# Late modulation in a transformer layer: the selecting matmul of each of 16 units is taken out, and the partial sums are added once by VectorE

## The reference

```
mod = silu(c) @ w_ada + b_ada                  # c: 1 prompt row and 8 sample rows, w_ada [1024, 6*1024]
sh1, sc1, gt1, sh2, sc2, gt2 = split(mod, 6)
h = rms_norm(x, norm1_g) * (1 + sc1) + sh1
proj = h @ w_in                                # retention q,k,v,g; attention q,k,v; gates
... retention (4 heads), differential attention (8 heads)
merged = gate_ret * (ret_o @ w_br_ret) + gate_diff * (diff_o @ w_br_diff)
x = x + gt1 * (merged @ w_out)
h2 = rms_norm(x, norm2_g) * (1 + sc2) + sh2
x = x + gt2 * hierarchical_moe(h2)
```

## Time and profile before

| what | value |
|---|---|
| three runs | 1525.07, 1530.54, 1531.76 us |
| median | 1530.54 us |
| profiled execution, first to last instruction | 1524.3 us |
| PE busy | 1495.9 us (98%), 7974 matmuls |
| DVE, ACT, POOL busy | 818.2, 652.8, 297.2 us |
| granted TensorE clock, mean | 0.998 |
| DMA | 301.88 MB, mean 198 GB/s |

### The profile page before, as it was taken

How to read it: one execution, slowest core, us unless ns; L and a number is a source line. 1 busy time by engine, 2 the same in 40 slices (tenths; PEclk the granted TensorE clock), 3 DMA queues, 4 the chain that set the end, 5 groups by cost and what they waited for, 6 DMA issues and landing times.

```text
span 1524.3 us, 21822 instructions
## 1 busy us (share of the span) xinstructions
PE 1495.9 (98%) x7974; PEld 1136.4 (75%) x7974; DVE 818.2 (54%) x1440; ACT 652.8 (43%) x1073; POOL 297.2 (19%) x177
## 2 busy tenths in 40 slices
PE   8999999999999999999999999999999999999998
PEld 6775777577757775778787667777788988887885
DVE  4332341234123412321585867755465799998998
ACT  5323211321232123312345454555333388888883
POOL 2342134213421342133100000000231100001004
PEclk9999999999999999999999999999999999999999
DMA  9545454645464546432432245134861699999996
GB/s 349 185 141 172 162 172 148 180 161 171 146 184 156 174 145 187 141 99 80 171 100 95 70 140 194 42 129 150 278 186 42 203 360 400 393 392 391 406 398 234
DMA packets 150221, 301.88 MB, mean 198 GB/s; under 512 B 16555, under 2 KB 44379, under 8 KB 149989
## 3 DMA queue, kind: packets, MB, share of 16 engines
q1 hardware_dynamic: 146310, 290.01, 55.4%
q0 software_dynamic: 3808, 10.49, 2.0%
HBM read 257.84 MB, written 45.77 MB: 199 GB/s over the span
## 4 chain that ended last, share of the span: by engine, by line
PE 44%; DMA 3%; DVE 2%; issue 1%; ACT 1%; POOL 0%; DVEq 0%; ACTq 0%; SPq 0%; POOLq 0%
PE pj L93 11%; PE pj L95 11%; PE pj L94 11%; PE d_B L2685 1%; DMA d_kc<-cache_diff_k 1%; PE d_B L2712 1%; PE d_B L2704 1%; DMA m_raw<-w 1%; PE d_B L2746 1%; PE d_B L2694 1%; PE d_B L2852 1%; PE d_B L2673 1%; PE d_B L1717 1%; PE pj L1709 0%; PE d_B L2723 0%
## 5 line engine op out<-in xcount | busy, mean ns | idle before, releaser
L93 PE MATMUL pj<-ring_hi,hT_hi 128*128 128x512 f32 x880 | 368.2, 418 | 3.0 <-ACT d_q_rows L2147 2.1
L95 PE MATMUL pj<-ring_hi,hT_lo 128*128 128x512 f32 x880 | 345.1, 392 | 0.0
L94 PE MATMUL pj<-ring_lo,hT_hi 128*128 128x512 f32 x880 | 344.4, 391 | 0.0
L511 POOL TENSOR_TENSOR ring_lo<-ring_raw,ring_hi 128x1024 fp32r<-128x1024 f32 x79 | 191.1, 2423 | 495.2 <-ACT ring_hi L585 495.2
L585 ACT ACTIVATE ring_hi<-ring_raw 128x1024 fp32r<-128x1024 f32 x79 | 83.3, 1057 | 362.3 <-DMA ring_raw<-w_in 349.5
L1577 DVE TENSOR_TENSOR m_lo<-m_raw,m_hi 128x1024 fp32r<-128x1024 f32 x188 | 221.9, 1220 | 17.2 <-ACT m_hi L1483 16.1
L93 PEld LDWEIGHTS pj<-ring_hi,hT_hi 128*128 128x128 f32 x880 | 166.1, 189 | 45.8 <-issue 12.4
L1483 ACT ACTIVATE m_hi<-m_raw 128x1024 fp32r<-128x1024 f32 x188 | 191.5, 1057 | 18.0 <-DMA m_raw<-w 14.9
L95 PEld LDWEIGHTS pj<-ring_hi,hT_lo 128*128 128x128 f32 x880 | 165.5, 188 | 36.7
L94 PEld LDWEIGHTS pj<-ring_lo,hT_hi 128*128 128x128 f32 x880 | 166.5, 189 | 28.4 <-issue 1.0
L782 DVE SCALAR_TENSOR_TENSOR r_S<-r_S,g,r_sm 128x512 f32<-128x512 f32 x64 | 45.0, 744 | 135.4 <-PE r_sm L1031 135.4
(11 more groups left out here) (386 smaller groups left out, 2410.9 us busy)
## 6 DMA issues: line engine op xcount, KB each, us to landing
m_raw<-w SPq DMA_DIRECT2D x188, 512.0 KB, 9.9
ring_raw<-w_in SPq DMA_DIRECT2D x72, 512.0 KB, 3.5
r_S<-state_ret SPq DMA_DIRECT2D x64, 256.0 KB, 4.5
r_ada_raw<-w_ada SPq DMA_DIRECT2D x16, 1024.0 KB, 6.6
o_state_s<-r_S SPq DMA_DIRECT2D x64, 256.0 KB, 4.3
a_raw<-w_ada SPq DMA_DIRECT2D x8, 1024.0 KB, 12.3
ring_raw<-w_in SPq DMA_DIRECT2D x32, 256.0 KB, 3.4
ring_raw<-w_br_ret SPq DMA_DIRECT2D x16, 512.0 KB, 4.2
```

The costliest lines, as they stand in the source:

```text
L93: pe.matmul(out, s_hi, m_hi, start=start, stop=False)
L94: pe.matmul(out, s_hi, m_lo, start=False, stop=False)
L95: return pe.matmul(out, s_lo, m_hi, start=False, stop=stop)
L511: pool.tensor_tensor(lo[:, p], raw[:, p], hi[:, p].bitcast(F32), ALU.subtract).then_inc(lo_done, 1)
```

## The change

- The job SP and all its parts go: the matmul `spread`, VectorE's `take_spread`, the 9 KB stores, and the two small loads of each unit (bias row, norm2_g).
- ACT copies all 128 rows of the unit's bank. SP stores these 128 x 256 partial sums to a scratch tensor (128 KB for each unit). ACT's copy of unit u waits for the store of unit u-2, which used the same buffer.
- SP sends the last unit behind the load of DQ0's piece 0. Behind the load of piece 1 it reads the partial sums back as 72 rows x 4 x 512 and loads b_ada and norm2_g nine times each, in 18 small DMAs (`load_parts`). GpSimd has filled the tile of factors with ones.
- VectorE adds the four strips and the bias in 5 operations of 72x512 (`sum_parts`), ahead of its five products for GR1. SP stores the result once, behind the load of DQ0's piece 3 (`store_mods`).
- The later phases read the same values from another layout. The tiles spr and g2 go, and some tiles lie elsewhere.

```diff
     def unit():
         u = next(ada)
-        return [("AD", u)], [("SP", u)]
+        return [("AD", u)]
...
-            ad, sp = unit()
-            jobs += ad + [("U", h - 1, u) for u in range(8, 16)] + sp
+            jobs += unit() + [("U", h - 1, u) for u in range(8, 16)]
             jobs += [("O", h - 1, t) for t in range(NT)]
             pieces.append(f"BR{h - 1}")
             banks += [(f"BR{h - 1}a", five), (f"BR{h - 1}b", five)]
-            for _ in range(2):
-                ad, sp = unit()
-                jobs += ad + sp
+            jobs += unit() + unit()
         if h == RH:
             break
-        ad, sp = unit()
-        jobs += ad + sp + [("T", h, t) for t in ROPE_ORDER]
+        jobs += unit() + [("T", h, t) for t in ROPE_ORDER]
...
-        spr = sb("r_spread", [P, 2, UW], F32)
-        g2 = sb("r_g2", [P, 2, UW], F32)
         uraw = sb("r_ada_raw", [P, KT, UW], F32)
+        sb.at = K.phase_base + 106496
...
+        MR = 9 * 4 * D_MODEL // W
+        parts = nc.alloc_sbuf_tensor_at("r_mod_parts", [P, NH, W], F32, offset=at_oT)
+        mod_add = nc.alloc_sbuf_tensor_at("r_mod_add", [P, W], F32, offset=at_oT + 8192)
+        mod_by = nc.alloc_sbuf_tensor_at("r_mod_by", [P, W], F32, offset=at_oT + 10240)
...
-                if u >= 2:
-                    job_taken(sp, "SP", u - 2)
-                sp.dma_start(mod[P - 1:P, u % 2], io["b_ada"][:, unit_cols(u)]).then_inc(ub_in[u % 2], 16)
-                c = unit_cols(u).start % D_MODEL
-                sp.dma_start(g2[0:9, u % 2], io["norm2_g"][:, c:c + UW].broadcast_to([9, UW])).then_inc(ub_in[u % 2], 16)
+
+            parts_home = io["mods"][1].rearrange("s p d -> (s p d)")
 
             def send_unit(u):
-                job_taken(sp, "SP", u)
-                seg, c = unit_cols(u).start // D_MODEL, unit_cols(u).start % D_MODEL
-                sp.dma_start(io["mods"][0, seg - 2, 0:9, c:c + UW], spr[0:9, u % 2]).then_inc(m_out[u % 2], 16)
+                job_taken(sp, "AD", u)
+                home = parts_home.rearrange("(p c) -> p c", p=P)
+                sp.dma_start(home[:, u * UW:(u + 1) * UW], mod[:, u % 2]).then_inc(m_out[u % 2], 16)
+
+            def load_parts():
+                for i in range(2):
+                    sp.wait_ge(m_out[i], 16 * NU // 2)
+                bank_done(sp, f"BR{RH - 1}b", NT - 1)
+                sp.wait_ge(by_set, 1)
+                home = parts_home.rearrange("(j p c) -> p j c", j=NH, c=W)
+                sp.dma_start(parts[0:MR], home[0:MR]).then_inc(parts_in, 16)
+                add = io["b_ada"][:, 4 * W:].rearrange("o (q c) -> (o q) c", c=W)
+                by = io["norm2_g"].rearrange("o (q c) -> (o q) c", c=W)
+                for r in range(9):
+                    sp.dma_start(mod_add[8 * r:8 * r + 8], add).then_inc(parts_in, 16)
+                    sp.dma_start(mod_by[8 * r + 4:8 * r + 6], by).then_inc(parts_in, 16)
+
+            def store_mods():
+                sp.wait_ge(mod_sum, 5)
+                sp.dma_start(io["mods"][0].rearrange("s p d -> (s p d)").rearrange("(p c) -> p c", c=W)[0:MR], mod_add[0:MR]).then_inc(mods_out, 16)
...
+                    elif was == "GR1":
+                        if p == 0:
+                            send_unit(NU - 1)
+                        elif p == 1:
+                            load_parts()
+                        elif p == 3:
+                            store_mods()
...
-            send_unit(NU - 1)
             sp.wait_ge(Sp_out, RH * 32)
             for i in range(2):
                 sp.wait_ge(S_out[i], 64 * 2 * RH)
-                sp.wait_ge(m_out[i], 16 * NU // 2)
+            sp.wait_ge(mods_out, 16)
...
-            pool.wait_ge(mod_zero, 1)
-            pool.memset(mod[96:P], 0.0).then_inc(mod_zero, 1)
-            pool.wait_ge(mod_zero, 2)
...
+                    if name == "GR1" and p == 3:
+                        bank_done(pool, f"BR{RH - 1}b", NT - 1)
+                        pool.memset(mod_by[0:MR], 1.0).then_inc(by_set, 1)
...
-                act.wait_ge(ub_in[u % 2], 32 * (u // 2 + 1))
-                act.activation(mod[0:105, u % 2], job_bank("AD", u)[0:105, 0:UW], ACT.Copy).then_inc(job_free("AD", u), 1)
+                if u >= 2:
+                    act.wait_ge(m_out[u % 2], 16 * (u // 2))
+                act.activation(mod[:, u % 2], job_bank("AD", u)[:, 0:UW], ACT.Copy).then_inc(job_free("AD", u), 1)
...
-            def take_spread(u):
-                job_done(dve, "SP", u)
-                if u >= 2:
-                    dve.wait_ge(m_out[u % 2], 16 * (u // 2))
-                src, dst = job_bank("SP", u)[0:9, 0:UW], spr[0:9, u % 2]
-                if unit_cols(u).start // D_MODEL == 4:
-                    ins = dve.scalar_tensor_tensor(dst, src, 1.0, g2[0:9, u % 2], ALU.add, ALU.mult)
-                else:
-                    ins = dve.tensor_copy(dst, src)
-                ins.then_inc(job_free("SP", u), 1)
+            def sum_parts():
+                dve.wait_ge(parts_in, 16 * 19)
+                a, b = parts[0:MR, 0], parts[0:MR, 2]
+                dve.tensor_tensor(a, a, parts[0:MR, 1], ALU.add).then_inc(mod_sum, 1)
+                dve.tensor_tensor(b, b, parts[0:MR, 3], ALU.add).then_inc(mod_sum, 1)
+                dve.wait_ge(mod_sum, 2)
+                dve.tensor_tensor(a, a, b, ALU.add).then_inc(mod_sum, 1)
+                dve.wait_ge(mod_sum, 3)
+                dve.tensor_tensor(a, a, mod_add[0:MR], ALU.add).then_inc(mod_sum, 1)
+                dve.wait_ge(mod_sum, 4)
+                dve.scalar_tensor_tensor(mod_add[0:MR], a, sel[0:MR, 9:10], mod_by[0:MR], ALU.add, ALU.mult).then_inc(mod_sum, 1)
...
-                    take_spread(u)
...
-                        take_spread(u + 1)
...
+                if j:
+                    sum_parts()
...
-            def spread(u):
-                job_taken(pe, "AD", u)
-                out = small("SP", u)
-                pe.matmul(out[0:9, 0:UW], sel[:, 0:9], mod[:, u % 2], start=True, stop=True).then_inc(sm_done, 1)
...
                 elif i == 4:
                     steps(h, 14)
                 elif i == 5:
-                    spread(u)
                     turn_o(h, 0)
...
             def in_branch(u, i):
                 if i % 4 == 1:
                     unit(u + i // 4)
-                elif i % 4 == 3:
-                    spread(u + i // 4)
 
             def in_v(h, u, i):
                 if i == 1:
                     unit(u)
-                if i == 3:
-                    spread(u)
                 if i >= 3:
                     turn_qk(h, ROPE_ORDER[i - 3])
...
+        mod_rows = io["mods"][0].rearrange("s p d -> (s p) d").rearrange("(r s) d -> r s d", s=4)
...
-                    sp.dma_start(gt1[:, 0], bc(io["mods"][0, 0, 0:1], [P, D_MODEL])).then_inc(gt1_in, 16)
+                    sp.dma_start(gt1[:, 0], bc(mod_rows[0:1, 0], [P, D_MODEL])).then_inc(gt1_in, 16)
...
+    sel[:, 2 * P + 9] = np.arange(P) // 2 % 4 == 2
```

More of the change, by code:

```diff
@@ L279, in phase_r @@
         tab_in, rope_in, S_in, S_out, Sp_out = sem("tab_in"), sem("rope_in"), many("S_in", 2), many("S_out", 2), sem("Sp_out")
-        u_in, ub_in, m_out = sem("unit_in"), many("unit_bias_in", 2), many("mods_out", 2)
+        u_in, m_out = sem("unit_in"), many("mod_parts_out", 2)
+        by_set, parts_in, mod_sum, mods_out = map(sem, ("mod_by_set", "mod_parts_in", "mod_sums", "mods_out"))
         roped, kd_done, z_done, qz_set = map(sem, ("qk_roped", "kd_done", "z_done", "qz_set"))
@@ L819, in _ @@
             dve.wait_ge(rope_in, 32)
-            u = 0
             for h in range(RH + 1):
@@ L847, in _ @@
                         add_branch(g, 1, t)
-                    take_spread(u + 2)
-                    u += 3
                 if h == RH:
@@ L863, in _ @@
                 else:
-                    take_spread(u)
                     for t in ROPE_ORDER:
                         take_T(h, t)
-                u += 1
                 for j in (4, 0, 1, 2, 3):
@@ L2061, in _ @@
                     job_done(sp, "O", 1, NT - 1)
-                    sp.dma_start(gt1[:, 0], bc(io["mods"][0, 0, 0:1], [P, D_MODEL])).then_inc(gt1_in, 16)
+                    sp.dma_start(gt1[:, 0], bc(mod_rows[0:1, 0], [P, D_MODEL])).then_inc(gt1_in, 16)
                     for b in range(DEC_B):
-                        sp.dma_start(gt1[b * DEC_L:(b + 1) * DEC_L, 1], bc(io["mods"][0, 0, b + 1:b + 2], [DEC_L, D_MODEL])).then_inc(gt1_in, 16)
+                        sp.dma_start(gt1[b * DEC_L:(b + 1) * DEC_L, 1], bc(mod_rows[b + 1:b + 2, 0], [DEC_L, D_MODEL])).then_inc(gt1_in, 16)
                 if name == "BR1" and m == 5:
@@ L2069, in _ @@
                 if name == "BR1" and m == 10:
-                    rows2 = lambda r, n: bc(io["mods"][0, 1:3, r].unsqueeze(0), [n, 2, D_MODEL])
+                    rows2 = lambda r, n: bc(mod_rows[r:r + 1, 1:3], [n, 2, D_MODEL])
                     sp.dma_start(mods[:, 0], rows2(0, P)).then_inc(mods_in, 16)
@@ L2088, in _ @@
```

(4 more changed lines are left out.)

## The result

| | before | after |
|---|---|---|
| median, lowest to highest, runs | 1530.02 us, 1525.07 to 1531.76, 4 | 1517.75 us, 1516.42 to 1518.34, 4 |
| ratio | | 0.9931 [0.9915, 0.9947] |
| span of the profiled execution | 1524.3 us | 1514.5 us |

The account below looks back on a forecast made before the run. PE, busy for 669 of 673 us in `phase_r`, was taken to bound that stage. The terms -6.0 - 5.6 + 1.1 = -10.5 us, off the median of 1530.54, gave 1520.0 us, with a range of 1512 to 1528.

Parts of the forecast that it names:

- Spreads in BR and V/QK: In `phase_r`, removing sixteen spread matmuls from PE saves 6.0 us in BR and 5.6 us in V and QK.
- the lower end: Smallest saving from the sixteen spreads in `phase_r`, at the stream's rate for their columns: 16 x 0.227 = 3.6 us.
- rival 1: At changes between steps PE's pause stays and only the columns go: 2.5 us gained, 1528.0 us; chance 10%.
- Other engines, stores, ACT's new wait: In `phase_r`, less work on other engines, larger stores and ACT's wait for unit u-2's store: 0 us.
- Nineteen DMAs: On SP's queue before DQ0's piece 2, at 0.47 us each: piece 2 2.6 us later, PE waits 1.1 us.
- The low end: Nineteen DMAs before DQ0's piece 2 at 0.30 us each: 5.7 us, piece 2 not late, cost 0.
- The chain behind the term (bank, slack, wait): At DQ0, late piece 2 delays ACT's split and reads of GR1's banks; PE waits beyond 1.5 us of slack.
- Sums in the shadow: VectorE's five sums, 3.1 us, run during GR1 and DQ0, end at about 707 and cost 0.
- Later phases shift as a whole: Behind `phase_r` everything waits for PE or the barrier, so later phases only move; the saving stays -10.5 us.
- rival 2: In the experts, a stream of loads that begins no earlier gives the gain back: 1530.5 us; chance 10%.
- Rival 3: Before DQ0 the nineteen DMAs take 1.40 us each and PE waits 18.7 us: +7.1, 1537.6 us; chance 5%.

Follow-up runs that it names:

- e1: Changed kernel with a matmul like the spread (256 columns, result unused) put back at all 16 places; 1530.56 us, 1.0004 of the kernel before.
- e3: Changed kernel with a one-record matmul in the stream's rounded format (128x128 weights, 256 columns) added at the 16 places; 1520.64 us.
- e7: Changed kernel with each unit's store made twice and ACT's copy waiting for both; 1513.74 us.
- e9: The changed kernel run again without an edit; 1516.12 us, 0.9920 of the kernel before.
- e5: Changed kernel with 20 more small loads behind the nineteen, ahead of the load of DQ0's piece 2; 1524.14 us.
- e6: Changed kernel with the eight outer-product jobs in G, which need the tile from memory, each one step later; 1512.81 us, 0.9902 of the kernel before.
- e4: The kernel before, unchanged, profiled once more; 1530.14 us, ratio 1.0005.
- e10: Changed kernel with the later steps of e6 and 47 instead of 36 filler matmuls at the start; 1511.55 us, 0.9885 of the kernel before.

## Why the prediction was right, and where it was not

- **Spreads in BR and V/QK (-6.0, -5.6): right.** The stage became shorter in steps of 0.75 and 0.69 us, 8 of each, 11.5 us; e1 brings the same 0.75 and 0.69 back. What was wrong is the reason given: not 0.227 us of columns and 0.5 of pause, but some 0.44 and 0.31. The rate of the stream was taken for an instruction that stands in the rows as x2 and whose records are 0.38 us for half the columns of a 0.39 us record; that was to be seen. The sum was not touched, since it went by the distance of starts. The bounds were: the lower end and the gain of rival 1, ahead of its 1.1 us of wait, should have been 16 x 0.44 = 7.0 us and not 3.6. Rival 1 itself is out by e3: another matmul at the same places makes no such pause.
- **Other engines, stores, ACT's new wait (0): right.** `phase_r` in e7, with the stores doubled, is as long as in e9, and ACT's longest wait ahead of a unit's copy in the profile after is 0.4 us, on PE's matmul and not on a store.
- **Nineteen DMAs (+1.1): the term that failed.** The step "I take 0.47 us each, as the nearest rows have" failed: they took 0.32 us each, 5.99 us in all, just below the 6.4 us that piece 2 leaves free behind piece 1. The low end, 0.30 us from the row of nine rows' norm_g, was the better neighbour, since it is the same sort of load in the same phase; the row taken was of another phase. The chain behind the term (bank, slack, wait) was right: in e5 piece 2 is 5.9 us late and PE waits 4.5; the slack of 1.5 us gives 4.4.
- **Sums in the shadow (0): right in place, not in time.** The forecast had them end at 707; the loads were done earlier, and they ended at 696.85, although one took 2.78 us.
- **Later phases shift as a whole: right.** The part behind the barrier is as long as before to 0.2 us. That it is so close is luck, since it varies by 3 us between profiles, but rival 2, which wanted the 11 us back there, is out.
- **Rival 3** needed 1.03 us per DMA. It had 0.32.

The stage gained 11.3 us against a forecast of 10.5. The wait of 1.1 us that wasn't there makes up the difference; the spreads gave 11.5 instead of 11.6, and 0.2 us between 11.5 and 11.3 stay unexplained. In the profile the start took 1.3 us of it back, which e9 doesn't show. That the ratio's 10.6 us nearly equal the forecast of 10.5 is luck: its interval is some 5 us wide, and the mis-sized term is smaller than that. The interval in e9 stands for 9.8 to 14.5 us, so the gain may well be larger than forecast.

## What to carry over

On a saturated TensorE, price an instruction by the distance of starts around it, at a place where nothing else stands, and not by columns. A small plain-float32 matmul with narrow weights in the middle of a stream in a rounded format costs several times its columns at the stream's rate (here 0.75 us for 256 columns, against 0.14 for one of the stream's own form), so work that sixteen of them do one by one is better left to an idle engine in one go. For small DMAs in a queue, count how many fit before the next load that someone waits for (here nineteen at 0.32 us in 6.4 us). Before comparing a stage between single profiles, take out the waits that scatter and the stretches at half the clock. And a step that waits for data from memory can be moved later instead of shortening the round trip.

## What the hardware showed that was not expected

**VectorE stood still beside GpSimd.** The fourth sum, which starts at 693.29, took 2.78 us while its like took 0.69. It started 0.37 us behind this instruction of GpSimd in the profile after, and ended 0.55 us behind its end:

```profile
692.92 2.60 POOL L531 TENSOR_TENSOR ring_lo<-ring_raw,ring_hi 128x1024 fp32r<-128x1024 f32 x1 [4.18 <-ACT ring_hi L605]
```

In e6 the same pair stands at 689.27 and 689.64, and the sum took 2.77 us; in e9 at 692.10 and 692.46, with 2.78. In e5 GpSimd had nothing to do at that moment, and VectorE's timeline has:

```profile
693.93 0.69 DVE L832 TENSOR_TENSOR r_mod_parts<-r_mod_parts,r_mod_add 72x512 f32<-72x512 f32 x1
```

The Trainium skill, "SBUF — State Buffer", section "SBUF: two separate sides", describes a pair of ports that VectorE and GpSimd share: an operation of VectorE with two inputs in SBUF and one of GpSimd that reads SBUF don't run side by side, and the later one is blocked until the earlier one ends. These four executions agree with that: the sum ended late in the three where GpSimd's operation stood beside it, and not in e5.

**A lower clock behind idle time of PE, but not by its length alone.** At the start 2.25 us without work were followed by a granted clock of 0.50, while behind 1.35 us (before) and 1.87 us (e3) it stayed at 1.00. In e5 4.5 us were followed by 0.50. But within `phase_r` a wait of 1.8 us was followed by 0.50 in e1, and one of 2.1 us in e4 by 1.00.

**A plain float32 matmul** is two records of 0.85 ns per column (the stream: one of 0.44). With full weights it hardly pauses in this stream (0.03 us); with nine columns of weights, whose load isn't done ahead, it costs some 0.31 us more.

**Left open:** why the loads of 8 and of 2 rows take 0.27 to 0.35 and 0.25 us on SP where those of the next phase take 0.43, what scatters the way through memory, when the clock falls behind a wait of about 2 us, why the load of narrow weights isn't done ahead, and whether e10's filler brings anything of its own.
